# First modulation and QKV projection in one stage, with shift and scale applied per partition behind the transposes

## The reference, cut to what is touched

```python
mod   = jax.nn.silu(c)     @ ada_w[i] + ada_b[i]      # latent tokens
mod_c = jax.nn.silu(c_ctx) @ ada_w[i] + ada_b[i]      # context tokens
h  = rms_norm(x,   norm1_g[i]) * (1 + sc1)  + sh1
hc = rms_norm(ctx, norm1_g[i]) * (1 + csc1) + csh1
q, k, v    = split(h  @ w_qkv)     # 1024 -> 1024 + 256 + 256 columns, rotary on q and k of h
qc, kc, vc = split(hc @ w_qkv)
```

## Time and profile before

| | |
|---|---|
| median of 3 runs | 2063.21 us (2056.62 to 2064.18) |
| the profiled execution | 2056.62 us, span 2054.8 us |
| busy: PE, PEld, DVE, ACT, POOL | 85%, 53%, 37%, 21%, 13% of the span |
| mean granted TensorE clock | 0.935 |
| DMA | 589.78 MB, mean 287 GB/s |

### The profile page before, as it was taken

The page is one execution under the profiler, slowest core; times in us unless marked ns, Lnnn a source line. Parts: engine busy times, 40 slices in busy tenths (PEclk is TensorE's granted clock), DMA queues, the critical chain, the costliest instruction groups (busy, mean ns, idle before and its releaser), DMA issues. The chain is left out here.

```text
span 2054.8 us, 33181 instructions
## 1 busy us (share of the span) xinstructions
PE 1738.8 (85%) x11192; PEld 1091.3 (53%) x11193; DVE 766.8 (37%) x1658; ACT 427.4 (21%) x789; POOL 271.8 (13%) x325
## 2 busy tenths in 40 slices
PE   3798989678999999999994699856669999999996
PEld 0677864435666666665662387212444555555553
DVE  1424552362222222222222754672334434343444
ACT  1213441101111111111111244770101111111111
POOL 1210000001111111111110160220011111111110
PEclk8899999798999999999997799987879999999998
DMA  7761024257999999999974653523649999999993
GB/s 271 239 238 71 1 100 185 78 206 298 414 418 417 414 415 408 401 396 401 389 292 192 265 129 110 183 84 154 278 161 420 419 417 418 414 414 415 417 417 125
DMA packets 122731, 589.78 MB, mean 287 GB/s; under 512 B 25731, under 2 KB 46841, under 8 KB 61233
## 3 DMA queue, kind: packets, MB, share of 16 engines
q1 hardware_dynamic: 95920, 510.20, 62.2%
q0 software_dynamic: 26608, 76.72, 10.1%
q10 hardware_dynamic: 144, 2.10, 0.2%
HBM read 586.75 MB, written 28.41 MB: 299 GB/s over the span
## 5 line engine op out<-in xcount | busy, mean ns | idle before, releaser
L1688 PE MATMUL ps<-m_wgu,m_xT 128*64 128x256 f32 x2944 | 330.6, 381 | 8.4 <-DMA m_wgu<-in_moe_w_up 6.8
L1688 PEld LDWEIGHTS ps<-m_wgu,m_xT 128*64 128x64 f32 x2944 | 252.4, 138 | 96.9 <-issue 37.3
L1946 PE MATMUL ps<-m_wgu,m_xT 128*64 128x256 f32 x2112 | 250.9, 385 | 4.3 <-DVE m_xT L2045 4.3
L1946 PEld LDWEIGHTS ps<-m_wgu,m_xT 128*64 128x64 f32 x2112 | 158.6, 138 | 98.4 <-issue 46.8
L1718 PE MATMUL ps<-mods,m_hidT 128*64 128x512 f32 x736 | 169.7, 602 | 30.8 <-ACT m_hidT L1740 20.3
L1782 DVE SCALAR_TENSOR_TENSOR m_hid<-m_act_g,m_meta,ps 128x256 f32<-128x256 f32 x46 | 22.1, 480 | 328.7 <-ACT m_act_g L1737 328.7
L2051 DVE TENSOR_TENSOR h<-h,ps 128x512 f32<-128x512 f32 x132 | 90.4, 685 | 124.4 <-PE ps L1935 123.4
L1979 PE MATMUL ps<-m_wd,m_hidT 128*64 128x512 f32 x528 | 120.6, 597 | 6.3 <-DMA m_wd<-in_moe_w_down 5.2
L1718 PEld LDWEIGHTS ps<-mods,m_hidT 128*64 128x64 f32 x736 | 58.4, 138 | 110.4 <-issue 110.4
L1886 POOL MEMSET h<- 128x1024 f32 x35 | 33.3, 952 | 521.9 <-PE ps L1924 404.4
L1632 POOL DMA_INDIRECT h<-h_rows,m_gidx x49 | 49.6, 1012 | 369.7 <-DVE m_gidx L1771 365.1
(11 more groups left out here) (425 smaller groups left out, 2844.4 us busy)
## 6 DMA issues: line engine op xcount, KB each, us to landing
m_wgu<-in_moe_w_gate SPq DMA_DIRECT2D x135, 1024.0 KB
m_wgu<-in_moe_w_up SPq DMA_DIRECT2D x135, 1024.0 KB, 11.7
mods<-in_moe_w_down SPq DMA_DIRECT2D x69, 1024.0 KB, 17.3
m_wd<-in_moe_w_down SPq DMA_DIRECT2D x66, 1024.0 KB, 9.0
c_rows<-y_rows SPq DMA_DIRECT2D x8, 2048.0 KB, 16.5
mods<-in_ada_w POOLq DMA_DIRECT2D x11, 1024.0 KB, 6.3
mods<-in_ada_w SPq DMA_DIRECT2D x11, 1024.0 KB, 4.8
mods<-in_lru_w_in SPq DMA_DIRECT2D x10, 1024.0 KB, 7.1
```

The costliest lines, as they stand in the source:

```text
L1688: last = pe.matmul(g.ps[half[s], GU, a * FE:(a + 1) * FE], xT[:, k, half[s]], wgu[:, bufs[s][0], bufs[s][1], a, k, :], start=(k == 0), sto ...
L1946: last = pe.matmul(g.ps[half[s], GU, a * FE:(a + 1) * FE], xT[:, k, half[s]], wgu[:, q, s, a, k, :], start=(k == 0), stop=(k == KD - 1))
```

## The change

`ada_phase` is gone; its work moves into the block of `qkv_phase`. In that block:

- SP loads `c`, `c_ctx`, then x and ctx (before: POOL's queue), then the 8 row blocks of `ada_w` (`ada0`, 7 buffers, so the last waits for the first projection), and right behind them the QKV weights. ACT issues the load of the table.
- The norm is `x * rstd` only, one `tensor_scalar` for each tile. `turn_rows(t)` is put behind projection step t + 1 on PE, in alternating pairs of banks; ACT and DVE copy the transposed rows to `xT` (one bank each).
- Behind the last projection step and `finish`, `turn_mods` turns the modulation rows into columns: 16 matmuls with 64 stationary columns and 4 moving ones each. DVE copies the 128x32 result to `mcol`. Nothing goes through HBM.
- `modulate(s, k)`: shift and scale per partition by one `tensor_scalar` on 128x256 (stream s, block k), 16 in all, on DVE. `rows_high` and `rows_low` are made 16 pieces of 128x256 read from SBUF (before: 8 each of 128x512 read from PSUM).
- ACT's order is: norms, `rows_out`, high parts of chunk 0, high part of chunk 1, then the 16 `rows_high`. DVE's order is: for each stream the modulation one block ahead of `rows_low`, the low parts of chunk 0 between the first stream's blocks and that of chunk 1 behind them, and then, behind both streams, the evacuations.
- The jobs' order starts (0,0) (0,1) (1,0) (1,1) (0,2) (0,3) (1,2) (1,3); from chunk 2 on it is as before. Job 0 waits for `rows_low` block by block, and so does the first job of the context tokens.
- POOL waits for the 8 projection steps before it clears kT (its space holds one of the loads), then issues the loads of the next modulation groups as before.

```diff
+                sp.dma_start(g.x[:, 0:LAT_TILES, :], ins["x"][0].rearrange("(t p) d -> p t d", p=P)).then_inc(x_in, 16)
+                sp.dma_start(g.x[:, LAT_TILES:TILES, :], ins["ctx"][0].rearrange("(t p) d -> p t d", p=P)).then_inc(x_in, 16)
+                for m in range(ada0.count):
+                    ada0.load(sp, m)
                 src = ins["attn_w_qkv"][0].rearrange("(p k) n -> p k n", k=KD)
-        jobs = [(c, t) for c in range(NCH) for t in range(TILES)]
+        jobs = [(c, 2 * s + t) for s in range(2) for c in range(2) for t in range(2)] + [(c, t) for c in range(2, NCH) for t in range(TILES)]
@@ scalar
+                act.dma_start(g.table[:], g.table_dram).then_inc(table_in, 16)
...
+                act.wait_ge(x_in, 32)
+                for t in range(TILES):
+                    norm.act(act, t)
+                for t in range(TILES):
+                    rows_out(t)
                 for n in range(WPARTS):
                     weights_high(n)
-                for t in range(1, TILES):
-                    rows_high(t)
-                    if t == 2:
-                        weights_high(part_of(1))
+                weights_high(part_of(1))
+                for s in range(2):
+                    for k in range(KD):
+                        rows_high(s, k)
@@ vector
+                def modulate(s, k):
+                    part = (slice(None), k, slice(s * SEQ, (s + 1) * SEQ))
+                    dve.tensor_scalar(xT[part], xT[part], mcol[:, k, 1, s:s + 1], mcol[:, k, 0, s:s + 1], ALU.mult, ALU.add).then_inc(h_mod, 1)
...
+                ada0.finish(dve, 0)
+                dve.wait_ge(cols_s, 1)
+                dve.tensor_copy(mcol[:].rearrange("p k m s -> p (k m s)"), g.ps[:, 6, 0:KD * 4]).then_inc(mcol_s, 1)
...
+                for s in range(2):
+                    modulate(s, 0)
+                    for k in range(KD):
+                        if k + 1 < KD:
+                            modulate(s, k + 1)
+                        rows_low(s, k)
+                        if s == 0 and k % KW == 0:
+                            weights_low(k // KW)
+                    if s == 0:
                         weights_low(part_of(1))
@@ gpsimd
+                ada0.load_small(pool)
+                pool.wait_ge(ada0.used, ada0.count)
                 pool.memset(kT[:], 0.0).then_inc(kz, 1)
                 pool.wait_ge(hturned, TILES)
                 ada.load_small(pool)
@@ tensor
+                def turn_mods():
+                    pe.wait_ge(ada0.ready, 1)
+                    picked = g.ident.rearrange("p (m c) -> p m c", m=2)
+                    for k in range(KD):
+                        for half in range(2):
+                            last = pe.matmul(g.ps[64 * half:64 * half + 64, 6, 4 * k:4 * k + 4], ada0.row[:, 0, k::KD],
+                                             picked[:, :, 32 * half:32 * half + 2], start=True, stop=True)
+                    last.then_inc(cols_s, 1)
...
+                for m in range(ada0.count):
+                    ada0.project(pe, m)
+                    if m == 1:
+                        pe.wait_ge(table_in, 16)
+                    if 1 <= m <= TILES:
+                        turn_rows(m - 1)
+                turn_mods()
```

More of the change, by code:

```diff
@@ L258, in wait_stored @@
         q.wait_ge(self.stored, 16 * 2 * self.TILES * (n + 1))
[L261 to L324, removed]
@@ L376, in qkv_phase @@
         sb = lambda n, s, d=F32: st.enter_context(nc.sbuf_tensor(n, s, d))
+        craw = sb("ada_craw", [P, 2, KD])
+        mcol = sb("n1_mcol", [P, KD, 2, 2])
         h_hi = sb("n1_h_hi", [P, KD, TOK], F32R)
@@ L385, in qkv_phase @@
         wide = lambda a: a.rearrange("p m d -> p (m d)")
+        xT = wide(g.mods[:, 4:8, :]).rearrange("p (k c) -> p k c", k=KD)
+        qk_w = wide(qk)[:, 0:2 * 2 * D].rearrange("p (q c) -> p q c", q=2)
+        ada0 = AdaGroups(g, "ada0", [(0, 0)], 5,
+                         [wide(g.mods[:, 0:2, :]), wide(g.mods[:, 2:4, :]), wide(g.mods_rest[:, 0:2, :]), wide(g.mods_rest[:, 2:4, :]),
+                          qk_w[:, 0, :], qk_w[:, 1, :], kT[:].rearrange("p a b c -> p (a b c)")],
+                         wide(v[:, 0:2, :])[:, None, :], wide(v[:, 2:4, :]))
         ada = AdaGroups(g, "ada1", [(0, 1), (0, 2)], 5, [wide(g.mods[:, 0:2, :]), wide(g.mods[:, 2:4, :]), wide(g.h[:, 2:4, :])],
@@ L396, in qkv_phase @@
         turned, turned_a, turned_v = g.sem("qk_turned"), g.sem("qk_turned_act"), g.sem("qk_turned_dve")
-        jobs = [(c, t) for c in range(NCH) for t in range(TILES)]
+        jobs = [(c, 2 * s + t) for s in range(2) for c in range(2) for t in range(2)] + [(c, t) for c in range(2, NCH) for t in range(TILES)]
+        through = lambda c: max(n for n, job in enumerate(jobs) if job[0] == c) + 1
         BANKS = 3
@@ L445, in _, with rows_out, rows_high @@
             def _(act):
-                def rows_high(t):
+                def rows_out(t):
                     act.wait_ge(hturned, t + 1)
-                    for b in range(2):
-                        act.activation(h_hi[:, 4 * b:4 * b + 4, t * P:(t + 1) * P],
-                                       g.ps[:, b, :].rearrange("p (k c) -> p k c", c=P), ACT.Copy).then_inc(h_high, 1)
+                    act.activation(xT[:, 0:KD // 2, t * P:(t + 1) * P],
+                                   g.ps[:, 2 * (t % 2), :].rearrange("p (k c) -> p k c", c=P), ACT.Copy).then_inc(rows_a, 1)
+                def rows_high(s, k):
+                    act.wait_ge(h_mod, KD * s + k + 1)
+                    part = (slice(None), k, slice(s * SEQ, (s + 1) * SEQ))
+                    act.activation(h_hi[part], xT[part], ACT.Copy).then_inc(h_high, 1)
                 def weights_high(n):
@@ L483, in _, with rows_low @@
                 chain = Chain(dve, chain_s)
[L485 to L490, removed]
+                def modulate(s, k):
+                    part = (slice(None), k, slice(s * SEQ, (s + 1) * SEQ))
+                    dve.tensor_scalar(xT[part], xT[part], mcol[:, k, 1, s:s + 1], mcol[:, k, 0, s:s + 1], ALU.mult, ALU.add).then_inc(h_mod, 1)
+                def rows_low(s, k):
+                    dve.wait_ge(h_high, KD * s + k + 1)
+                    part = (slice(None), k, slice(s * SEQ, (s + 1) * SEQ))
+                    dve.tensor_tensor(h_lo[part], xT[part], h_hi[part].bitcast(F32), ALU.subtract).then_inc(h_split, 1)
                 def weights_low(n):
@@ L496, in weights_low @@
                                       w_hi[:, c % 2, k0:k1, :].bitcast(F32), ALU.subtract).then_inc(lo_s, 1)
[L498 to L503, removed]
+                dve.memset(g.cs[:], 0.0).then_inc(cs_clear, 1)
+                dve.memset(g.eps[:], EPS).then_inc(consts, 1)
+                dve.memset(g.ones_bf[:], 1.0)
+                dve.memset(g.ones[:], 1.0)
+                dve.wait_ge(x_in, 32)
+                for t in range(TILES):
+                    dve.wait_ge(norm.rooted, t + 1)
+                    chain.link(dve.reciprocal(g.rstd[:, t:t + 1], g.root[:, t:t + 1]))
+                    dve.tensor_scalar(g.h[:, t, :], g.x[:, t, :], g.rstd[:, t:t + 1], None, ALU.mult).then_inc(norm.ready, 1)
+                dve.wait_ge(table_in, 16)
+                dve.tensor_copy(g.ident_bf[:], g.ident)
+                dve.tensor_copy(g.mask_bf[:], g.field("mask"))
+                dve.tensor_copy(g.before_bf[:], g.field("before"))
+                for t in range(TILES):
+                    dve.wait_ge(hturned, t + 1)
+                    dve.tensor_copy(xT[:, KD // 2:KD, t * P:(t + 1) * P],
+                                    g.ps[:, 2 * (t % 2) + 1, :].rearrange("p (k c) -> p k c", c=P)).then_inc(rows_v, 1)
+                ada0.finish(dve, 0)
+                dve.wait_ge(cols_s, 1)
+                dve.tensor_copy(mcol[:].rearrange("p k m s -> p (k m s)"), g.ps[:, 6, 0:KD * 4]).then_inc(mcol_s, 1)
+                dve.wait_ge(mcol_s, 1)
+                dve.wait_ge(rows_v, TILES)
+                dve.wait_ge(rows_a, TILES)
+                for s in range(2):
+                    modulate(s, 0)
[6 more added lines that the diff above has]
+                    if s == 0:
                         weights_low(part_of(1))
@@ L509, in _ @@
                 for n, (c, t) in enumerate(jobs):
-                    if c and t == 0 and c + 1 < NCH:
+                    if c and c + 1 < NCH and n == (through(0) if c == 1 else TILES * c):
                         weights_low(part_of(c + 1))
```

32 lines of the change are left out of this document (21 added, 11 removed).

## The result

| | before | changed |
|---|---|---|
| median | 2062.96 us, 4 runs (2056.62 to 2064.18) | 2042.02 us, 4 runs (2040.56 to 2047.53) |
| profiled execution | 2056.62 us, span 2054.8 us | 2040.56 us, span 2038.7 us |
| mean granted clock | 0.935 | 0.934 |

The ratio of the times is 0.9905, with a 95% interval of 0.9886 to 0.9924: about 20 us less.

What follows compares the result with a forecast made beforehand. Stages in a row with barriers leave PE little work for 28.4 us before job 0. Gains of 15.1 us up to job 3 and 4.6 behind it sum to 19.7: 2063.2 - 19.7 = 2043.5 us median, range 2036 to 2053.

Steps and rivals of the forecast that it cites:

- gain at job 7: Eight QKV jobs end 19.7 us earlier: 15.1 at job 3's start and 4.6 more behind it.
- The front: Up to the last projection: bound by DMA, first block lands at 15.9, end unchanged at 35.7 us, upper end 39.9.
- Rival (a): Cold front: PE stays at 1.2 GHz through the projections, loss of 2 to 4 us, 2046.5; chance 0.17.
- The columns: 32 instructions of `turn_mods` behind `finish` take 3.5 us, bounds 2.0 to 6.5; first block handed over at 41.6.
- The lower bound: For `turn_mods`: each instruction costs a quarter of a transpose, 0.06 us, giving 2.0 us.
- The wait that took the place of the one removed: Rows on ACT wait for chunk 1, landed at 43.6, high part done at 45.9; bounds 42.4 and 48.
- The 240 GB/s: Rate of chunks 0 and 1 in 512 B pieces: 2.1 MB take 8.7 us, 33.8 to 42.5.
- DVE's pace: From the first rows DVE's work sums to 16.5 us, so job 3 starts at 62.4; bounds 14.5 and 19.1.
- the 0.22 of my lower bound: DVE's modulations at 0.22 us each, giving a lower bound of 14.5 us for DVE's work.
- Behind job 3: First `ada` step no longer waits for its DMA; job 3 to job 7 takes 17.9 instead of 22.6 us, 4.6 gained.
- the forward shift behind job 7: From job 7's end to the span's end nothing may differ by more than 2 or 3 us.
- The range: 2036 to 2053 us, from the better and worse rivals with the runs' own scatter of 3 us.

Runs made afterwards that it cites:

- kernel 10: Changed kernel with the four token tiles transposed behind projection steps 4 to 7 instead of 1 to 4; job 3 started at 61.69 us, 0.5 later.
- kernel 2: Changed kernel, but POOL's small loads and next groups' first loads wait for chunk 1's high part; job 3 at 60.58 us, job 7 evacuated at 78.80.
- kernel 1: Changed kernel with chunk 1's high part written on ACT behind the latent tokens' 8 pieces; job 3 at 56.74 us, job 7 evacuated at 76.45.
- kernel 4: Changed kernel with the old order of the first eight jobs; job 3 at 61.65 us, job 7 evacuated at 79.88, no change counted from chunk 1.
- kernel 5: Changed kernel with modulation columns stored to HBM and loaded back instead of turned on TensorE; job 3 at 69.06 us, job 7 evacuated at 88.79.
- kernel 8: Changed kernel, but POOL issues the next groups' 1 MB loads only after job 3; job 7 evacuated at 83.72 us, 4.29 later.
- kernel 11: Changed kernel with the edits of kernel 1 and kernel 3 together; 2037.5 us, ratio 0.9874 to the kernel before, job 7 evacuated at 72.00.
- kernel 3: Changed kernel with four PSUM banks for the jobs instead of three; job 7 evacuated at 78.32 us, 1.11 earlier.
- kernel 9: Kernel before, but POOL issues two of the next groups' 1 MB loads ahead of its wait for transposes; job 3 at 84.12 us, job 7 evacuated at 102.33.
- kernel 6: Kernel 5 with POOL's loads also waiting until the columns have landed; job 3 at 61.80 us, job 7 evacuated at 80.03.
- kernel 7: Kernel 5 with chunk 1's high part behind the latent rows, as in kernel 1; job 3 at 71.09 us, job 7 evacuated at 90.83.

## Why the prediction was right

Predicted 2043.5 us, measured 2042.0. That the two medians meet within 1.5 us is partly luck, since four runs of the changed kernel lie 7 us apart; the marks are the better evidence, and the way there holds step by step, to within 1.8 us:

| step | predicted | measured |
|---|---|---|
| last projection ends | 35.7 | 35.40 |
| first block modulated | 41.6 | about 39.8 |
| chunk 1 landed | 43.6 | 42.60 |
| its high part done, rows begin | 45.9 | 44.42 |
| job 3 | 62.4 | 61.19 |
| job 3 to job 7 | 17.9 | 18.2 |
| gain at job 7 | 19.7 | 20.7 |

**The front.** The DMAs bound it as told, the first block landing at 16.07 (15.9 predicted). Rival (a) did not come, but not for the reason that I gave. I had the level rise because steps and transposes leave PE almost no hole; it rose within step 1 (1.66), before the first transpose at 20.05, and in kernel 10 without any transpose there (1.55). In the other nine profiles with this front it rose a little later, between the end of step 1 and step 2 (1.30 in kernel 2, the latest). What is new is that steps 0 and 1 are 2.4 us apart and work follows at once, where all but the last two steps of the kernel before are 3.7 to 4.5 us apart and all take 1.93. What the transposes do is to hold the level: without them it fell within step 4 of kernel 10. The last step was again at the lower level (1.93 us) in this profile; in kernels 1, 4, 5, 8, 10 and 11 it took 1.06 or 1.07. By the rule of the Trainium skill (TensorE: Matmul & The Clock Gate, Part 4) transposes don't count for the clock and the last projection would have ended at 39.9; the last projection ended at 35.40 here. Kernel 10 speaks against the rule itself, since its clock came back between 27.57 and 30.63, in a stretch that is 1.97 us of transposes and one step, while the steps alone before it had lost it, and steps alone 3.7 us and more apart never had it in the kernel before. That is one such stretch in one profile.

**The columns.** 32 instructions took 2.09 us, 65 ns each, at a granted clock of 0.50; my 3.5 lay too near the upper bound. The lower bound, a quarter of a transpose at the lower clock, met it by luck: in kernels 1 and 8 the same 32 instructions took 2.09 us too, although the granted clock was 1.00 until 37 us, so their time doesn't go with the clock as a transpose's does (1.97 and 1.16). PE in kernel 1:

```profile
35.99 2.09 PE L558 MATMUL ps<-table,v 128*64 128x4 f32 x32 [1.61 <-DVE v L245]
```

The 1.4 us had no effect behind the wait for chunk 1.

**The wait that took the place of the one removed.** This was the step that mattered most, and kernel 1 proves it: it cost 5.6 us at the rows and 4.45 at job 3. Its terms were off in two ways that partly cancel. The 240 GB/s was a misreading: rows 6 show 230 and 305, whose mean is 267. In the changed kernel the pieces of 512 B, queued ahead of time, moved at 290:

```profile
34.00:36.00 2.00, 1.41 (x8) 0.00 (x0) 0.46 (x1) 1.26 (x2) 0.50 (x1) 0.50 1.22 293
```

So 2.1 MB take 7.2 us instead of 8.7. On the other side, the 2 us between the last byte and the landing (kernel 2) are no term of my sum. From the last block's landing at 33.47 to chunk 1's at 42.60 are 9.1 us, where I had 9.8.

**DVE's pace.** 16.5 us predicted from the first rows on, 16.8 measured (44.42 to 61.19). Modulations and `rows_low` followed each other after 0.33 us, as assumed; the 0.22 of my lower bound had no row and didn't come. Kernel 3 shows that the bank was all that tied PE to DVE ahead of job 3.

**Behind job 3.** 4.6 us predicted; the measured 18.2 us leave 4.4 of the first profile's 22.7, kernel 8 gave 4.29 back, and kernel 9, with early loads in the kernel before, took 18.2 as well.

**Where the text was wrong.** It called the forward shift behind job 7 rigid to 2 or 3 us. The order of work is, the durations aren't: the profiles differ by up to 10 us there. The range had 3 us of scatter on either side and the forecast was on the median, which was right, but a reader who had compared the two profiled spans alone would have found 16 us. I also counted the early loads as a free effect of the change. They are one only because of when they are issued (kernel 9).

**What each part of the change is worth,** at the marks: the new order of jobs nothing; the columns on TensorE 0.6 to 1.2 us over a lean trip through HBM (7.9 us where that trip meets POOL's loads, kernel 5); loads of the next groups 4.3 us. The rest, some 15 to 16 us, is shift and scale no longer broadcast and no longer needed ahead of the transposes, with norm and transposes under the loads. That remainder is what is left over, not a run of its own.

## What to carry to other kernels

When a round trip is removed, look for what the same engines had queued ahead of the work that it released: here a weight conversion that stood first in ACT's program kept 4.5 us of the gain at job 3, and one moved line gave it back, of which 3.0 reached job 7. An engine that is freed sooner stands longer at its next wait, and on TensorE a longer stand can also cost the clock (here 1.5 us behind waits of 2.00, 2.68 and 3.09 us, nothing behind 1.78 and 1.83), so one more buffer at that wait can be worth more together with the first edit than alone (7.4 us instead of 2.98 and 1.11). Time marks inside the changed stage, not the whole, when an effect is smaller than the scatter of everything behind it.

## What the runs showed of the hardware that I had not expected

- A transfer counted as landed about 2 us after the DMA engines had gone quiet (13 GB/s in 40 to 42 us, landing seen at 41.98).
- Four loads of 4 KB took 8.2 us each (median) beside 1 MB loads of another queue, and 1.7 with POOL's loads out of the way (kernels 5 and 6). The Trainium skill (DMA: Bandwidth & Descriptors, Queues, rings and completion order) says that each DMA engine takes turns between queues, a packet at a time; that fits, if a turn of long rows is long, which no run here shows directly.
- Conversely, pieces of 512 B lose against rows of 8 KB: parts of a chunk that otherwise come 1 us apart came 5.9 us apart.
- 32 small fp32 matmul instructions (64 stationary columns, 4 moving) took 2.09 us at a granted clock of 0.50 and at 1.00 alike (kernels 1 and 8).
- The clock fell behind a wait of only 2.00 us (kernel 7) and stayed behind one of 1.83 (kernel 6).
- The granted clock of the first 30 us stands at 1.00 in the windows of the kernel before, yet each of its first-stage matmuls took 1060 ns; in the changed kernel the same line goes from 1.94 us a step to 1.07 within windows that all show 1.00. In kernel 9 the column still shows 1.00 from 56 to 70 us, where tiles of transposes took 1.94 and 1.97 us. Early in a trace the durations tell the level, not the clock's column.
